# SSD step order, feed-forward evictions and the first odd attention part in a two-layer hybrid block

## The reference

```python
z, xbc, dt_raw = split(u @ w_in)
xbc = silu(causal_dwconv(xbc, conv_w, conv_b))
xs, b_in, c_in = split(xbc)
dt = softplus(dt_raw + dt_bias)
...  # chunked scan: y_diag (within chunks) + y_off (carried state)
hg = (y + xs * d_skip) * silu(z)
hg = hg * rsqrt(mean(hg * hg over a group of 512 channels) + eps) * gate_g
return hg @ w_out
```

## Time and profile before

| | |
|---|---|
| median of 3 runs | 2463.39 us |
| lowest, highest | 2460.68, 2467.31 us |
| the profiled execution | 2468.59 us |
| its span | 2466.5 us |
| TensorE busy | 2274.3 us, 92% |
| VectorE busy | 1280.1 us, 52% |
| GpSimd busy | 1010.0 us, 41% |
| ScalarE busy | 921.3 us, 37% |
| mean granted TensorE clock | 0.96 |

### The profile page before, as it was taken

One profiled execution on the slowest core, in us unless ns is written; L12 is line 12 of the kernel. 1 busy time (PEld: TensorE's weight loads), 2 busy tenths in 40 slices (PEclk: granted clock), 3 DMA queues, 4 the chain that ended last, 5 costly groups with the idle time before them and its releaser, 6 DMA issues.

```text
span 2466.5 us, 38755 instructions
## 1 busy us (share of the span) xinstructions
PE 2274.3 (92%) x15968; PEld 1982.6 (80%) x15968; DVE 1280.1 (52%) x1919; ACT 921.3 (37%) x1480; POOL 1010.0 (41%) x905
## 2 busy tenths in 40 slices
PE   6889899888999999999998999998998899997887
PEld 6778888778999999985598989976785478885665
DVE  6575757588725735234368716732113551016773
ACT  4362626343313333336532323332224431225661
POOL 3252534334545540022244455544345543435751
PEclk9889998989999999999999999999998999998999
DMA  3111112111222222220012222222221011520100
GB/s 154 52 68 53 69 52 69 52 52 69 76 99 93 83 91 95 85 86 1 1 69 70 86 99 97 78 100 74 84 102 70 18 69 69 156 103 35 35 1 34
DMA packets 29373, 175.59 MB, mean 71 GB/s; under 512 B 3984, under 2 KB 4496, under 8 KB 12304
## 3 DMA queue, kind: packets, MB, share of 16 engines
q1 hardware_dynamic: 29200, 173.14, 19.9%
HBM read 166.71 MB, written 2.10 MB: 68 GB/s over the span
## 4 chain that ended last, share of the span: by engine, by line
PE 68%; DVE 9%; POOL 7%; issue 7%; ACT 2%; POOLq 2%; DVEq 2%; SPq 1%; DMA 0%; ACTq 0%
PE PS L683 20%; PE PS L684 19%; PE PS L685 19%; POOL ring_r L2336 2%; PE PS L960 2%; DVE arena L1815 1%; POOL ring_r L2345 1%; POOL arena L2427 1%; POOL arena L2465 1%; ACT arena_r L1306 1%; DVEq L396 1%; POOLq L2462 1%; PE PD L990 1%; POOL uT L2439 1%; PE PC L960 1%
## 5 line engine op out<-in xcount | busy, mean ns | idle before, releaser
L685 PE MATMUL PS<-arena_r,ring_r 128*128 128x264 f32 (+3 forms) x3728 | 1144.9, 307 | 0.0
L2336 POOL TENSOR_TENSOR ring_r<-ring,arena_r 128x512 fp32r<-128x512 f32 (+1 forms) x456 | 596.1, 1337 | 881.3 <-ACT arena_r L1306 881.3
L685 PEld LDWEIGHTS PS<-arena_r,ring_r 128*128 128x128 f32 x3728 | 714.9, 192 | 31.1
L683 PE MATMUL PS<-arena_r,arena_r 128*128 128x264 f32 (+3 forms) x2288 | 691.6, 302 | 25.7 <-issue 8.8
L684 PE MATMUL PS<-arena_r,arena_r 128*128 128x264 f32 (+2 forms) x2256 | 676.1, 300 | 0.0
L683 PE MATMUL PS<-arena_r 128*128 128x264 f32 (+3 forms) x1792 | 566.0, 316 | 22.2 <-DVEq L396 9.3
L683 PEld LDWEIGHTS PS<-arena_r,arena_r 128*128 128x128 f32 x2288 | 435.3, 190 | 53.7 <-issue 25.5
L684 PE MATMUL PS<-uT_r,arena_r 128*128 128x264 f32 (+2 forms) x1472 | 470.0, 319 | 0.0
L684 PEld LDWEIGHTS PS<-arena_r,arena_r 128*128 128x128 f32 x2256 | 429.7, 190 | 13.0 <-issue 0.2
L1306 ACT ACTIVATE arena_r<-ring 128x2048 fp32r<-128x2048 f32 (+1 forms) x146 | 262.0, 1795 | 419.8 <-PE PS L685 404.8
L683 PEld LDWEIGHTS PS<-arena_r 128*128 128x128 f32 x1792 | 348.4, 194 | 50.8 <-issue 21.4
(11 more groups left out here) (329 smaller groups left out, 2827.2 us busy)
## 6 DMA issues: line engine op xcount, KB each, us to landing
ring<-stream SPq DMA_DIRECT2D x130, 1024.0 KB, 4.8
ring<-down SPq DMA_DIRECT2D x32, 704.0 KB, 4.0
hT<-x_in SPq DMA_DIRECT2D x4, 528.0 KB, 7.2
arena<-tables SPq DMA_DIRECT2D x4, 512.0 KB, 3.8
arena<-arena SPq DMA_DIRECT2D x16, 128.0 KB, 2.4
out<-uT SPq DMA_DIRECT2D x4, 512.0 KB, 2.8
par<-params SPq DMA_DIRECT2D x1, 1634.5 KB, 13.9
arena<-arena SPq DMA_DIRECT2D x8, 136.0 KB, 3.3
```

What stands on the lines that cost most here:

```text
L683: mm(out_, r32(ah), r32(bh), start=start, stop=False)
L685: return mm(out_, r32(a), r32(bh), start=False, stop=stop)
L2336: last = G.tensor_tensor(r32(low[:, cut]), raw[:, cut], split(high[:, cut]), ALU.subtract)
```

## The change

1. `dt` owns no tile any more; its product goes to the bank PD, with a semaphore of its own. B's projection of group 0 stands ahead of `stat`.
2. In group 0, z 1 stands ahead of `l0`.
3. From group 1 on, z 0 stands ahead of the last pair of the group before; the group then starts with bt and gram, ga and low 3, l0, z 1, gs, two xt, rc, z 2, xt, z 3.
4. In the last group z 3 stands ahead of the states, and two instead of three output projections stand between them.
5. In the feed-forward, `scale` evicts a tile; unit r + 1's gate tile is evicted behind unit r's convolutions, its value tile between two `normalised` calls.
6. `ODD`'s first two entries change places.

```diff
@@ ssd_order
+        then = [("z", g + 1, 0)] if g + 1 < GROUPS else []
...
-        return out + [("pair", g, HPG // 2 - 1)]
+        return out + then + [("pair", g, HPG // 2 - 1)]
...
-    order = [("dt", 0, 0), ("stat", 0, 0)] + projections(0) + [("dtt", 0, 0), ("z", 0, 0), ("end", 0, 0)]
-    order += [("bt", 0, 0), ("gram", 0, 0), ("l0", 0, 0), ("z", 0, 1), ("xt", 0, 0), ("xt", 0, 1), ("xt", 0, 2)]
+    order = [("dt", 0, 0), ("B", 0, 0), ("stat", 0, 0)] + projections(0)[1:] + [("dtt", 0, 0), ("z", 0, 0), ("end", 0, 0)]
+    order += [("bt", 0, 0), ("gram", 0, 0), ("z", 0, 1), ("l0", 0, 0), ("xt", 0, 0), ("xt", 0, 1), ("xt", 0, 2)]
...
-        order += z[0] + [("ga", g - 1, 0), ("low", g - 1, 3), ("bt", g, 0), ("gs", g - 1, 0), ("gram", g, 0), ("l0", g, 0)]
-        order += [("rc", g - 1, 0)] + z[1] + [("xt", g, 0), ("xt", g, 1)] + z[2] + [("xt", g, 2), ("spread", g, 0), ("spread", g, 1)]
+        order += [("bt", g, 0), ("gram", g, 0), ("ga", g - 1, 0), ("low", g - 1, 3), ("l0", g, 0)] + z[1] + [("gs", g - 1, 0)]
+        order += [("xt", g, 0), ("xt", g, 1), ("rc", g - 1, 0)] + z[2] + [("xt", g, 2), ("spread", g, 0), ("spread", g, 1)]
+        order += z[3]
         if last:
-            order += [("decay", g, 0)] + states(g, dict(enumerate(s[0:3])))
-            order += through(g, {0: z[3], 1: s[3], 2: s[4], 3: s[5], 5: s[6], 7: s[7]})
+            order += [("decay", g, 0)] + states(g, {0: s[0], 2: s[1]})
+            order += through(g, {0: s[2], 1: s[3], 2: s[4], 3: s[5], 5: s[6], 7: s[7]})
...
-OFF_TILE = ("spread", "decay", "weigh", "carry", "low", "ga", "gs", "rc", "stat")
+OFF_TILE = ("spread", "decay", "weigh", "carry", "low", "ga", "gs", "rc", "stat", "dt")
+ODD[0], ODD[1] = ODD[1], ODD[0]
@@ dt: TensorE, VectorE
-                            last = mm(t[0:32, V0 + a:V0 + b], w_dt[:, k, :], hT[:, k, a:b], start=k == 0, stop=k == KD - 1)
-                    last.then_inc(ps_full, 1)
+                            last = mm(dt_sums[0:32, a:b], w_dt[:, k, :], hT[:, k, a:b], start=k == 0, stop=k == KD - 1)
+                    last.then_inc(sem("dt_full"), 1)
...
-                    dve.wait_ge(ps_full, dt_M + 1)
+                    dve.wait_ge(sem("dt_full"), 1)
@@ low 2, VectorE
                         V.tensor_tensor(GA, squares(g, 0), squares(g, 1), ALU.add)
+                        dve.drain()
@@ ffn_dve
+                def scale(r, m):
+                    dve.drain()
+                    tile_wait(dve, f"ffn{i}a", 0, 2 * R, 2 * r + m)
+                    v0 = first_column(width)
+                    V.tensor_tensor(ffn[("rawg", "rawv")[m]][:, FCONV - 1:FCONV - 1 + width],
+                                    tile_of(f"ffn{i}a", 2 * r + m)[:, v0:v0 + width], rstd[:, 0:width], ALU.mult)
+                    signal(dve, free_of(f"ffn{i}a", 2 * r + m))
+                scale(0, 0)
...
+                        early = half == 0 and r + 1 < FIRST
...
+                            elif (r, m) == (0, 1):
+                                scale(r, m)
...
+                        if early:
+                            scale(r + 1, 0)
                         dve.wait_ge(sem("glu"), n0 + r + 1)
...
-                        if half == 0 and r < 2:
+                        if early:
                             normalised(4 * r)
+                            scale(r + 1, 1)
                             normalised(4 * r + 2)
@@ odd attention, VectorE, ahead of the loop
-            odd_sum(0)
-            for n in range(2):
-                odd_scale(n)
+            odd_scale(0)
+            odd_sum(1)
```

More of the change, by code:

```diff
@@ L122, in ssd_order @@
         s = [[("s", g - 1, m)] for m in range(8)]
-        order += z[0] + [("ga", g - 1, 0), ("low", g - 1, 3), ("bt", g, 0), ("gs", g - 1, 0), ("gram", g, 0), ("l0", g, 0)]
-        order += [("rc", g - 1, 0)] + z[1] + [("xt", g, 0), ("xt", g, 1)] + z[2] + [("xt", g, 2), ("spread", g, 0), ("spread", g, 1)]
+        order += [("bt", g, 0), ("gram", g, 0), ("ga", g - 1, 0), ("low", g - 1, 3), ("l0", g, 0)] + z[1] + [("gs", g - 1, 0)]
+        order += [("xt", g, 0), ("xt", g, 1), ("rc", g - 1, 0)] + z[2] + [("xt", g, 2), ("spread", g, 0), ("spread", g, 1)]
+        order += z[3]
         if last:
-            order += [("decay", g, 0)] + states(g, dict(enumerate(s[0:3])))
-            order += through(g, {0: z[3], 1: s[3], 2: s[4], 3: s[5], 5: s[6], 7: s[7]})
+            order += [("decay", g, 0)] + states(g, {0: s[0], 2: s[1]})
+            order += through(g, {0: s[2], 1: s[3], 2: s[4], 3: s[5], 5: s[6], 7: s[7]})
         else:
             B, C, x0, x1, x2, x3 = ([p] for p in projections(g + 1))
-            order += z[3] + [("decay", g, 0)] + states(g, {0: s[0], 1: s[1] + B, 2: s[2], 3: s[3] + C})
+            order += [("decay", g, 0)] + states(g, {0: s[0], 1: s[1] + B, 2: s[2], 3: s[3] + C})
             order += through(g, {0: s[4] + s[5], 1: s[6], 2: s[7], 3: x0, 4: x1, 5: x2, 7: x3})
@@ L431, in build @@
         sums = PC[:, :, :].rearrange("p a b -> p (a b)")[:, V0:V0 + L]
+        dt_sums = PD[:, :, :].rearrange("p a b -> p (a b)")[:, V0:V0 + L]
         def x_of(g):
@@ L1791, in dve_step @@
                     dve.drain()
-                    dt_M = SSD_M["dt", 0, 0]
                     dtv, dtt, dt = (ssd_dt[n][0:32, :] for n in ("dtv", "dtt", "dt"))
-                    dve.wait_ge(ps_full, dt_M + 1)
-                    V.tensor_tensor(dtv, PS[dt_M % 2][0:32, V0:V0 + L], rstd[0:32, :], ALU.mult)
+                    dve.wait_ge(sem("dt_full"), 1)
+                    V.tensor_tensor(dtv, dt_sums[0:32, :], rstd[0:32, :], ALU.mult)
                     dve.drain()
                     V.tensor_scalar(dtv, dtv, prm("dt_bias", 32), None, ALU.add)
-                    signal(dve, sem("dtv_full"), ps_free[dt_M % 2])
+                    signal(dve, sem("dtv_full"))
                 elif what in ("B", "C", "x"):
```

## The result

| | before | after |
|---|---|---|
| median, beside each other on one chip | 2462.98 us (4 runs) | 2438.38 us (4 runs) |
| lowest, highest | 2460.68, 2467.31 | 2435.08, 2439.81 |
| profiled execution, its span | 2468.59, 2466.5 | 2435.08, 2433.0 |
| mean granted clock of that execution | 0.960 | 0.968 |

The ratio is 0.9899 (95% interval 0.9879 to 0.9918): the change is faster, by 24.6 us. The median of 2438.4 lies in the range, 8.7 us above the predicted 2429.7, at rival B's value.

What follows compares the result with a forecast made beforehand. TensorE was taken as the bound, idle 192 us of 2466.5, so only idle time and clock could change. The terms -0.8 + 5.0 + 16.6 - 4.5 + 8.8 + 6.6 + 2.0 = 33.7 gave 2429.7 us; range 2418 to 2446.

Steps and rivals of the forecast that it cites:

- rival B: New waits of 1 to 2 us among short products each bring a half-clock projection: 8.5 us less gain, 2438; chance 0.12.
- Start: B's projection ahead of the statistics: 1.0 us gained, 1.8 lost to the clock, -0.8 (bounds -2.7 and +1.1).
- Group 0: Second gate projection ahead of the first-chunk decays removes their 3.74 us wait; transposes come earlier: +5.0 (bounds +3.7 and +6.5).
- Group starts: Starts of groups 1, 2, 3 reordered around the gate projections: 3.5, 5.2 and 7.9 us gained, sum +16.6.
- clock -4.5: Charge for reduced clock behind three new waits at the group starts, 1.5 us each: -4.5 (bounds 0 and -8).
- rival A: Waits move with the work: decays' product stands as long at group starts, reciprocal comes out of cover; 2446; chance 0.18.
- The wait of 1.9 us in place of 2.93: Group 2's start: decays' product waits 1.9 us for ScalarE's copies, replacing the 2.93 us wait for the squares' sum.
- rival D: Slower: GpSimd's remainders fall on VectorE's binding stretches, doubling convolution passes; with 48 further passes 43 us lost, 2473; chance 0.04.
- Last group: Projection 3 before the states readies the weight remainders early, removing TensorE's 5.66 us wait: +8.8 (bounds +5.7 and +10).
- Feed-forward: Earlier evictions remove the first stall; VectorE still binds; fifth unit starts 3.3 us earlier, twice: +6.6 (bounds +2 and +19).
- Odd attention: Pair part 0 first fills the 7.39 us idle of the compressed blocks' chain, which itself gets later: +2 (bounds -1, +4).

Runs made afterwards that it cites:

- the fill: Changed kernel plus unused matrix products in TensorE's waits before groups 2 and 3's first gate projection and groups 1 to 3's decays' product: 2429.9 us, ratio 0.9870.
- SSD-only kernel: Changed kernel with feed-forward and odd attention put back as before, leaving only the SSD parts of the change: 2442.0 us, ratio 0.9920.
- the one with feed-forward and odd alone: Kernel before with only the feed-forward evictions and the odd attention's exchange changed: 2457.6 us, ratio 0.9977.
- the changed kernel with the cut: Changed kernel with GpSimd's weight remainders cut to 16 columns per piece in both feed-forwards' first halves, omitting some low remainders: 2419.5 us, ratio 0.9817.

## Why the prediction came out as it did

The order of the waits and most terms held, and the time fell in the range. But the clock was charged at less than half of its price, so that group 2 came out as long as before, and the feed-forward term was read from an unlucky execution.

- **Start (-0.8).** The wait before the third unit is 6.16 us ("about 6"), the square root comes about 1 us earlier, the stretch is 0.5 us longer in the pair of profiles. Right within what the clock moves it.
- **Group 0 (+5.0).** 6.7 us by the stretch of 19.8 to 13.1, inside the bounds but for 0.2 (5.3 to 6.8 over all profiles): projection 1 took 6.7 us (78.45 to 85.12) where I had it half cold at 7.3, and the decays' product behind it 0.96.
- **Group starts (+16.6, clock -4.5).** The walk was right: with the clock held by the fill, the three stretches take 323.0 us against 341.2 (338.5 in the other profile with the old order), 15.5 to 18.2 less. The charge was the failed step. I put 1.5 us at each of three new waits, 4.5 in all; the fill shows 10.0 to 13.1. Two reasons: the projections behind the decays' waits paid 1.6, 2.7 and 2.0 us over 5.9, and the short products between wait and projection paid too (the decays' product took 1.43 and 1.88 us in groups 2 and 3, 0.96 at clock 1.00 in group 0); and the wait of 2.12 us before the pair did not vanish when the gate projection took its place. The walk had it there, since the projection needs the same tile, but put no clock behind it (286.3 to 292.2 is 5.9 us); it stands (2.18, 2.75) and pays 1.6 in each of two groups. This is rival B in its place, at more than its price. Of the 12.1 us that the two terms promise 4.7 came, so by the time alone this place is as near to rival A, which had nothing here; what speaks for B is the fill.
- **The wait of 1.9 us in place of 2.93.** Predicted with its cause, ScalarE's order; measured 1.55, 2.32 and 2.40. The excess in groups 2 and 3 is VectorE's product doubled under GpSimd, rival D's mechanism at one instruction. No gate projection shows the reciprocal as its releaser: rival A's second half did not come.
- **Last group (+8.8).** 46.4 (46.1) to 38.3 (38.2): 8.1, with the 5.66 gone. From its first pair to the feed-forward's statistics about 1 us goes back (65.0 and 64.1 to 65.7 and 65.6), which I had not looked at.
- **Feed-forward (+6.6).** The fifth unit starts at 53.3 us behind the statistics in the changed kernel (52.2 to 54.4 over the kernels with its feed-forward code), exactly where the walk put it (598.3 in the old trace is 53.3 behind its statistics). The step that failed is the comparison: the 601.64 of the earlier trace rows held a fourth unit at reduced clock. That unit in the kernel before, and in the SSD-only kernel with the same feed-forward code:

```profile
588.63:601.64 13.01, 13.01 (x97) 0.89 0.23 81
```

```profile
568.65:580.36 11.71, 11.70 (x96) 1.00 0.25 90
```

  There the fifth unit starts at 54.7 us, and the change is worth 1.3 and 1.5 us in the two stretches instead of 3.3 each; between the kernel before and the one with feed-forward and odd alone it is 0.8 and 1.3. I had also expected one stall before the fifth unit's, and there are two, of 1.96 and 2.03 us, beside its own of 2.57.
- **Odd attention (+2.0).** 7.39 us became 1.71 + 3.57, not 3. The blocks' transposes start 36.6 us behind the first product of the compressed blocks' MLP instead of 35.8: the chain got later, as walked. Over the whole stretch to the end the new order takes 263.2 to 265.0 us, the old 264.0 and 264.7: about 1 us or nothing.

By their places: 0 + 6.7 + 4.7 (mean of 341.2 and 338.5, less that of 336.1 and 334.1) + 8.1 - 1.1 + 2.8 + 0.7 = 22, of the 24.6 measured. The pair of profiles also holds 4.2 us that belong to no term: the stretch from the attention's statistics to the second feed-forward's takes 332.4 us before and 330.8 after, that from the even layer's to the odd one's 343.6 and 341.0, though the change touches neither. They are not the change's, for the fill kernel, with all of it, takes 343.2 in the second, and in the attention the changed kernel with the cut is 3.6 us behind the changed kernel 165 us after the statistics. How the rest of the gain divides between the start, the odd attention and such chances stays open; each is below what these runs tell.

## What to carry to other kernels

A stall is worth its length only where the clock behind it is the same before and after, so price a wait that stays among short products nearer to the dearest half-clock row in the trace than to the cheapest, and ask of each step put into a stall whether it waits for the same thing. Read a term of a few us from two profiles of the same code before taking it at its face: one half-clock unit in the one execution that was profiled was worth 1.3 us in each feed-forward here. Where one engine's list holds a copy that frees a tile behind work that waits for another engine, move the step that makes the tile: it was worth 8 to 10 us here, as much as the filler (the two intervals overlap), and adds no product.

## What was not expected of the hardware

Products whose results nobody reads hold the granted clock as well as real ones: 16 of them in a wait of 2.2 to 2.8 us brought the next projection from 0.77 and 0.79 to 1.00, and 44 in the 6.16 us of the start brought the third unit's first projection from 0.73 to 1.00. The length of a wait alone does not tell what it costs. Before gate projection 1, waits of 0.41 to 1.09 us were followed by clock 1.00 and one of 1.20 by 0.78. But at 40.43 in the changed kernel 1.47 us between two long projections were followed by 1.00, and at 92.30 a wait of 0.76, with 0.50 and 0.83 us of waiting among short products just ahead of it, by 0.73. Nor does the same stall always cost the same: 2.57 us of waiting before the fifth unit were followed by a unit of 13.00 us at 0.89 in one kernel and of 11.70 at 1.00 in another, with the same instructions:

```profile
597.81:610.81 13.00, 13.00 (x96) 0.89 0.36 147
```

```profile
579.30:591.00 11.70, 11.70 (x96) 1.00 0.32 122
```

A GpSimd piece cut to 16 columns no longer doubles a VectorE pass: with the cut the mean of the 176 passes is 762 ns, and 831 and 882 without it. Operations with one input from SBUF are slowed too, the copy into the high part (L2039) from 922 to 1218 ns; the scaled evictions from PSUM (L2025) take 701 ns in either case.
